# Two hybrid transformer blocks on one core: the compressed branch and the gates between the q, k, v units, the mixing norm's root applied by the consumers, two open output units

## The reference, cut to what matters

```python
x = x + 0.5 * swiglu_ffn(rmsnorm(x, ffn1_norm_g), ffn1_w_in, ffn1_w_out)
h = rmsnorm(x, mix_norm_g)
q, kv, nsa_g, conv_in, q_mem, merge_g = jnp.split(h @ w_in, split_points, axis=-1)
q = rmsnorm(q.reshape(b, s, N_HEADS, HEAD_DIM), q_norm_g)
kc, vc, ks, vs, kw, vw = [t.reshape(...) for t in jnp.split(kv, 6, axis=-1)]
k_cmp = rmsnorm(compress(kc, cmp_pe_k, cmp_w1_k, cmp_w2_k), k_norm_g)   # silu((blocks + pe) @ w1) @ w2
v_cmp = compress(vc, cmp_pe_v, cmp_w1_v, cmp_w2_v)
gates = jax.nn.sigmoid(nsa_g)
o_nsa = nsa_attention(q, k_cmp, v_cmp, rmsnorm(ks, k_norm_g), vs, rmsnorm(kw, k_norm_g), vw, gates, rel_bias)
o_conv = short_gated_conv(conv_in, conv_w, conv_b)     # gate_b * (conv3(gate_c * x_in) + conv_b)
o_mem = memory_attention(q_mem, mem, ...)
g_nsa, g_conv, g_mem = jnp.split(jax.nn.sigmoid(merge_g), 3, axis=-1)
x = x + (g_nsa * o_nsa + g_conv * o_conv + g_mem * o_mem) @ w_out
x = x + 0.5 * swiglu_ffn(rmsnorm(x, ffn2_norm_g), ffn2_w_in, ffn2_w_out)
```

## Time and profile before

| | |
|---|---|
| median of 3 runs | 2926.3 us (2925.95 to 2928.32) |
| the profiled execution | 2924.95 us |
| its span in the profile | 2923.1 us |
| TensorE matmul busy | 2858.3 us, 98% of the span |
| VectorE, ScalarE, GpSimd busy | 1254.6, 1156.1, 1110.9 us |
| mean granted TensorE clock | 0.991 of full |

### The profile page before, as it was taken

One profiled execution on the slowest core, in us unless ns is written; L12 is line 12 of the kernel. 1 busy time (PEld: TensorE's weight loads), 2 busy tenths in 40 slices (PEclk: granted clock), 3 DMA queues, 4 the chain that ended last, 5 costly groups with the idle time before them and its releaser, 6 DMA issues.

```text
span 2923.1 us, 33800 instructions
## 1 busy us (share of the span) xinstructions
PE 2858.3 (98%) x13586; PEld 2282.5 (78%) x13586; DVE 1254.6 (43%) x2039; ACT 1156.1 (40%) x1817; POOL 1110.9 (38%) x506
## 2 busy tenths in 40 slices
PE   8999989899999999999999999999999899999999
PEld 6888867777777887888887777888887567888887
DVE  4333244354555246333334435433337555533323
ACT  4232233355654453322224544332235455332323
POOL 3444433022224524444432213444443333444443
PEclk9999999899999999999999999999999999999999
DMA  4443232122212312222321112223322242222322
GB/s 146 152 137 125 93 111 87 51 82 78 83 65 101 114 61 93 95 100 97 109 83 58 58 51 80 94 101 105 107 86 87 81 129 94 94 101 95 118 91 80
DMA packets 83364, 275.55 MB, mean 94 GB/s; under 512 B 14183, under 2 KB 20583, under 8 KB 82568
## 3 DMA queue, kind: packets, MB, share of 16 engines
q1 hardware_dynamic: 73292, 257.10, 25.7%
q0 software_dynamic: 9440, 15.16, 1.5%
q10 hardware_dynamic: 476, 1.12, 0.1%
HBM read 271.13 MB, written 10.58 MB: 96 GB/s over the span
## 4 chain that ended last, share of the span: by engine, by line
PE 89%; DVE 6%; ACT 3%; issue 1%; DMA 1%; SPq 0%; POOL 0%; DVEq 0%; ACTq 0%
PE bank L442 20%; PE bank L443 20%; PE bank L444 20%; PE bank L597 5%; PE bank L601 5%; PE bank L599 5%; PE bank L624 1%; PE bank L829 1%; PE bank L663 1%; PE bank L651 1%; DVE tmp L1620 1%; PE bank L798 1%; PE bank L968 1%; DMA raw<-in_w 1%; PE bank L859 1%
## 5 line engine op out<-in xcount | busy, mean ns | idle before, releaser
L2178 POOL TENSOR_TENSOR w_lo<-raw,w_hi 128x1024 fp32r<-128x1024 f32 (+1 forms) x423 | 1073.5, 2541 | 1656.6 <-ACT w_hi L1119 1656.6
L1119 ACT ACTIVATE w_hi<-raw 128x1024 fp32r<-128x1024 f32 (+1 forms) x424 | 469.5, 1108 | 1267.2 <-PE bank L444 1133.8
L442 PE MATMUL bank<-a_hi,w_hi 128*128 128x512 f32 x1760 | 696.4, 396 | 19.5 <-DVE a_lo L1602 7.2
L444 PE MATMUL bank<-a_lo,w_hi 128*128 128x512 f32 x1760 | 686.9, 390 | 0.0
L443 PE MATMUL bank<-a_hi,w_lo 128*128 128x512 f32 x1760 | 686.9, 390 | 0.0
L442 PEld LDWEIGHTS bank<-a_hi,w_hi 128*128 128x128 f32 x1760 | 331.7, 188 | 101.1 <-issue 12.2
L443 PEld LDWEIGHTS bank<-a_hi,w_lo 128*128 128x128 f32 x1760 | 331.6, 188 | 71.9 <-issue 4.5
L444 PEld LDWEIGHTS bank<-a_lo,w_hi 128*128 128x128 f32 x1760 | 331.6, 188 | 69.2
L597 PE MATMUL bank<-a_hi,w_hi 128*128 128x512 f32 x704 | 284.7, 404 | 1.9 <-issue 0.8
L601 PE MATMUL bank<-a_lo,w_hi 128*128 128x512 f32 x704 | 282.2, 401 | 0.0
L599 PE MATMUL bank<-a_hi,w_lo 128*128 128x512 f32 x704 | 277.2, 394 | 0.0
(11 more groups left out here) (314 smaller groups left out, 3475.1 us busy)
## 6 DMA issues: line engine op xcount, KB each, us to landing
raw<-in_w SPq DMA_DIRECT2D x360, 512.0 KB, 3.4
raw<-in_w SPq DMA_DIRECT2D x64, 704.0 KB, 4.0
bias_rows<-bias_table POOLq DMA_DIRECT2D x4, 2048.0 KB, 29.4
strip<-bias_rows SPq DMA_DIRECT2D x16, 448.0 KB, 4.2
cw<-in_cw POOLq DMA_DIRECT2D x4, 1024.0 KB, 5.5
terms<-forget_cumsum SPq DMA_DIRECT2D x8, 512.0 KB, 8.0
terms<-forget_cumsum SPq DMA_DIRECT2D x8, 384.0 KB, 6.7
x<-in_x_t SPq DMA_DIRECT2D x4, 512.0 KB, 7.6
```

Source lines behind the costliest of these rows:

```text
L442: mm(dst, high[:, w], hi[:, kbase + b], start=start and b == 0, stop=False)
L444: last = mm(dst, high[:, w], lo[:, kbase + b], start=False, stop=stop and b == nk - 1)
L1119: act(w_hi[v % 3][:, 0:nk * P], raw[v % 5][:, 0:nk * P], ACT.Copy).then_inc(sem("w_hi_ready"), 1)
L2178: eng.tensor_tensor(w_lo[v % 5][:, 0:nk * P], raw[v % 5][:, 0:nk * P], w_hi[v % 3][:, 0:nk * P].bitcast(F32), ALU.subtract).then_inc(sem(" ...
```

## The change

It has five parts.

1. **Norm.** `updated` and `update` of `ffn0_out` get the norm name "mix": VectorE writes x·gain, ScalarE `a_hi` and VectorE `a_lo` in the update of each chunk. The root stays in `rstd`, and every consumer multiplies its tile by it on VectorE: the q, k, v and `cc` tiles, the gates, the convolution tiles, `qmem`, `gnsa` and `gmem`. The root of the memory norm moves to `raw_t[1]`, and so does the square of `rstd` for the convolution.
2. **Order.** The stage `qkv0` is written out by hand in `block_qkv` on each engine, with `cc` tiles first, and the host lays the weights in that order. The two hidden layers of `compress` and its small matmuls stand between the units.
3. **Gates.** They are computed transposed: 24 matmuls of 512 columns with 48 weight columns, sigmoid, and four small transposes.
4. **Position term.** Two operations of 128x992 with two tensor inputs in place of 16 of 128x124.
5. **Output units.** `wo0` opens two units: 21 matmuls of the first, 21 of the second, then the rest.

```diff
+                project_tile(0)
+                second = unit_steps(u + 1, bank[1][:, :], a_hi, a_lo)
+                advance(second, 9)
+                mean("mix")
+                advance(second)
+                for t in range(2, 4):
+                    project_tile(t)
+                hidden(0)
+                project_tile(4)
+                key_raw()
+                project_tile(5)
+                head_mean(0)
+                key_mean()
+                project_tile(6)
+                head_mean(1)
+                hidden(1)
+                project_tile(7)
...
+                def hidden(kv):
                     eng.wait_ge(sem("xc_ready"), kv + 1)
+                    if kv == 1:
+                        eng.wait_ge(sem("kcmp_done"), 2)
...
+                def gate_raw():
+                    eng.wait_ge(sem("wg_split"), 1)
+                    eng.wait_ge(sem("vcmp_done"), 2)
+                    for b in range(NCH):
+                        w = slice(b * 48, (b + 1) * 48)
+                        mm(bank[7][0:48, :], wg_hi[:, w], a_hi[:, b], start=b == 0, stop=False)
...
+            def merged_out():
...
+                first, second = out(0), out(1)
+                advance(first, 21)
+                advance(second, 21)
+                advance(first)
+                advance(second)
+                for k in range(2, NCH):
+                    advance(out(k))
...
-            mean("mix")
-            project("qkv0", a_hi, a_lo, parts=split_base["mix_norm"])
-            small(v0["qmem"], wg_hi, wg_lo, 48, "wg_split", "gates_raw")
-            compress()
+            block_qkv()
             nsa()
...
-                updated(f"ffn{f}_out", (None, "attn0", "ple0", "ple1")[f])
+                updated(f"ffn{f}_out", ("mix", "attn0", "ple0", "ple1")[f])
...
-                        eng.wait_ge(sem("unit_done"), u + t + 1)
+                        if name == "qmem":
+                            eng.wait_ge(sem("qmem_seen"), t + 1)
+                        else:
+                            eng.wait_ge(sem("unit_done"), u + t + 1)
                         act(act_t[sq % 2][:, 0:n], bank[t % 4][:, 0:n], ACT.Square).then_inc(sem("square_ready"), 1)
...
+                        if name == "qmem":
+                            wait("unit_done", u + t + 1)
+                            eng.tensor_tensor(b[:, 0:n], b[:, 0:n], rstd[:, :], ALU.mult).then_inc(sem("qmem_seen"), 1)
+                        if ended:
+                            normed()
                         group.append(t)
...
+                for g in range(2, 5):
+                    seen(g)
+                    normed(g - 1)
+                eng.tensor_tensor(rstd_twice[:, :], rstd[:, :], rstd[:, :], ALU.mult)
+                gate_seen()
...
+                def conv_gate(c):
+                    wait("unit_done", u + 4 * c + 1)
+                    eng.tensor_tensor(cb[:, :], bank[6][:, :], rstd[:, :], ALU.mult).then_inc(sem("conv_taken_even"), 1)
+
+                def conv_gate_seen(c):
+                    wait("unit_done", u + 4 * c + 4)
+                    eng.tensor_tensor(bank[7][:, :], bank[7][:, :], rstd[:, :], ALU.mult).then_inc(sem("conv_gate_seen"), 1)
...
+                    own(eng.tensor_tensor(cu[:, 2:S + 2], cu[:, 2:S + 2], rstd_twice[:, :], ALU.mult))
```

More of the change, by code:

```diff
@@ L335, in build @@
         }
+        block_norms = [t for t, tile in enumerate(tiles["qkv0"]) if tile[0] == "norm"]
+        block_turns = [bank[6], bank[7], bank[7], bank[5]]
         norm0, sq0, v0, g, n, v = {}, {}, {}, 0, 0, 0
@@ L532, in project, with block_qkv, project_tile, head_mean @@
                 post()
[L534 to L552, removed]
+            def block_qkv():
+                u, tk = U0["qkv0"], taken0["qkv0"]
+                def project_tile(t):
+                    eng.wait_ge(sem("tile_taken"), tk + t - 3)
+                    unit(u + t, 0, bank[t % 4][:, :], a_hi, a_lo, K8,
+                         parts=split_base["mix_norm"] if t == 0 else None).then_inc(sem("unit_done"), 1)
+                def head_mean(g):
+                    if g >= 2:
+                        eng.wait_ge(sem("tile_taken"), tk + block_norms[g - 2] + 1)
+                    eng.wait_ge(sem("square_ready"), g + 1)
+                    mm(bank[4 + g % 2][:, :], cst("mean_head"), act_t[g % 2][:, :], start=True, stop=True)\
+                        .then_inc(sem("head_mean"), 1)
+                def hidden(kv):
                     eng.wait_ge(sem("xc_ready"), kv + 1)
+                    if kv == 1:
+                        eng.wait_ge(sem("kcmp_done"), 2)
                     for half in range(2):
@@ L563, in compress @@
                         last.then_inc(sem("cw1_used"), 1)
[L564 to L581, removed]
@@ new lines, in value_raw @@
+                def value_raw():
+                    eng.wait_ge(sem("chid_ready"), 4)
+                    for g in range(4):
+                        for ht in range(2):
+                            last = mm(bank[6 + g % 2][32 * (g % 2):32 * (g % 2) + NCMP, g // 2 * HD:(g // 2 + 1) * HD],
+                                      chid[:, ht, g, :], cw2[:, 1, ht, :], start=ht == 0, stop=ht == 1)
+                    last.then_inc(sem("vcmp_raw"), 1)
+                def gate_raw():
[4 more added lines that the diff above has]
+                        mm(bank[7][0:48, :], wg_hi[:, w], a_hi[:, b], start=b == 0, stop=False)
+                        mm(bank[7][0:48, :], wg_lo[:, w], a_hi[:, b], start=False, stop=False)
+                        last = mm(bank[7][0:48, :], wg_hi[:, w], a_lo[:, b], start=False, stop=b == NCH - 1)
+                    last.then_inc(sem("gates_raw"), 1)
@@ new lines, in block_qkv @@
+                head_mean(3)
+                gate_raw()
+                project_tile(9)
+                head_mean(4)
+                gate_turn()
+                project_tile(10)
+                eng.wait_ge(sem("gates_ready"), 1)
+                block_turn_v(0)
+                project_tile(11)
+                block_turn_v(1)
+                for t in range(12, 19):
+                    project_tile(t)
+                    head_mean(t - 7)
+                project_tile(19)
+                block_turn_v(2)
@@ L1092, in _ @@
             mem_attention()
-            tiles_by_four("wo0", b_hi, b_lo, "x_done", x0["wo0"], split_base["gmem"])
+            merged_out()
             ffn(1, "ffn1")
```

394 lines of the change are left out of this document (277 added, 117 removed).

## The result

The changed kernel takes 2897.23 us (median of 4 runs, 2897.01 to 2897.79), the kernel before 2927.24 (4 runs, 2925.95 to 2928.32). The ratio is 0.9899, with a 95% interval of 0.9884 to 0.9914: 30 us less. The forecast was 2893, in a range of 2885 to 2902. Its net is right, and more so than its parts: one of them came out at nothing, and within another two errors cancelled.

What follows compares the result with a forecast made beforehand. TensorE, working 98% of the span, was taken as the bound, with time to come from its waits, slow stretches and removed work. The terms summed to -33.0 us, giving a forecast of 2893 us in a range of 2885 to 2902.

Steps and rivals of the forecast that it cites:

- Mixing norm, -16.0: From ffn0_out's last matmul to unit 1: 22.3 us shrink to 6.32, one unit and one mean without idle time.
- Gates, -17.3: Gate matmuls: 23.1 us including the wait become 24 matmuls at 5.44 plus about 0.3 for four small transposes.
- Compressed branch, -2.7: Both hidden layers and small matmuls: 24.25 us become 21.5, including a new 3.9 us stall before the second layer.
- the rival in which it falls to the low clock: First hidden layer's 64 matmuls take 12.0 us instead of 7.0, plus 1.5 in the unit behind: 2900; chance 0.10.
- v turns, -0.7: Turns of the v tiles between unit 1 and the gates: units now standing between hide most of 0.8 us waiting.
- Output units, -3.9: At wo0, 42 matmuls needing only earlier chunks cover the wait for the last b_lo and its low clock; 0.2 left.
- qmem, +7.6: In qmem, ScalarE's squares wait behind VectorE's 16 memory-input operations: unit 4 comes 4.6 us later, then 3.0 more.
- The rival of held squares: In qmem, VectorE's memory-input squares stay held 2.2 us each, so the head mean comes 4.4 later: 2897; chance 0.10.
- The sentence that the clock falls in every such stall: For PE's stalls: the clock falls in each too, so a removed wait gives back more than its own length.
- nsa and the queues at nothing: nsa's three added VectorE multiplications per chunk hide behind waits for PE; DMA queues issue the same transfers: no cost.

Runs made afterwards that it cites:

- the early `xc`: Changed kernel with VectorE making the values' xc right behind the last cc tile, and wg_lo moved behind kcmp: 2890.05 us.
- `gates_narrow`: Changed kernel with the gates' 24 matmuls of 512 columns replaced by the former 96 of 48 columns, at the new place: 2910.1 us.
- `third_in_norm`: Changed kernel with memory-input squares spread behind qmem multiplications 0 to 2, and multiplication 3 moved behind the first operation of the first pair's norm: 2889.18 us.
- `best`: Changed kernel with spread memory-input squares, early xc, kcmp ahead of wg_lo, multiplication 3 within the norm, and kcmp and vcmp clearings moved earlier: 2882.76 us.
- `combined`: Changed kernel with early xc, all 16 memory-input operations behind the second qmem multiplication, and the position term in 16 operations again: 2893.06 us.

## Why the prediction was right, and where it wasn't

- **Mixing norm, -16.0: right.** No idle time at the mean, and 33 matmuls ahead of it, as priced. Put back ahead of unit 0, the mean alone costs 6.7 of it.
- **Gates, -17.3: nearly.** The 24 matmuls take 5.98 us (460.82 to 466.80) where I had 5.44, and the turns 0.37. The reason given, the wait and the low clock that it brings, was the smaller part of it: without any wait ahead the old shape still took 15.4 us.
- **Compressed branch, -2.7: this step was mis-sized; it came to 0.** The second layer's stall was 5.10, not 3.9, and outside its bounds of 1.7 and 4.5. The chain was the right one, and `wg_lo` was held as assumed; the error is the `xc` pair at 3.6 instead of 2.4. I priced it by width, from contiguous operations. The layer then took 9.55 for 9.05. And the stall of 1.34 ahead of the first layer wasn't in the sum at all. There the `xc` pair (400.79 to 406.5) was held by a `w_lo` for 2.0 us; at 3.68 it would have ended at 404.5, before TensorE was free at 405.2. The layer itself took 7.2, so the rival in which it falls to the low clock did not occur.
- **v turns, -0.7: right.** The three turns inside the block add 0.4 to 0.5 us each, with the unit behind them, and the fourth, now in `nsa`'s first chunk, 0.5: 1.9 us, as the forecast left them, where there were 2.6.
- **The rest of the block.** It took 153.3 us (382.4 to 535.69) where the terms give 149.4. The branch is 2.7 of the 3.9, the gates 0.6; most of the rest lies in units of about 5.6 us instead of 5.44 behind a change of the kind of matmul.
- **Output units, -3.9: right**, -3.6.
- **qmem, +7.6: right in its first mechanism, and in size, 7.7, partly by luck.** 3.48 us at the head mean were forecast as 3.5, and VectorE's operations on the memory input were not held any more. The rival of held squares did not occur. But the 1.3 us of low clock behind that stall were absent: mean and next unit took 7.28 us, and 7.21 before. So unit 4 came 3.7 late and not 4.6, and the second half, 3.0 by a guess between bounds, was 4.0: the new wait of 2.23 at unit 6, and 1.6 of low clock behind it. The two errors cancel. In the second execution of the same kernel the low clock stood behind the head mean and not at unit 6: 4.3 and 2.4, 6.7 in all. The sentence that the clock falls in every such stall was wrong. For the second half the runs gave the place: multiplication 3 behind the first pair's norm.
- **nsa and the queues at nothing: right.**
- **The sum.** -16.0 - 16.8 + 0 - 0.7 - 3.6 + 7.7, with about 0.4 of other small losses, is some -29 us; the profiled executions differ by 27.2, which holds 1.9 of lateness at the start, and the medians by 30.0.

## What to carry to other kernels

When work moves from a chain that everything waits for into each consumer, list what already stands in the consumer engine's program at that point. Here one multiplication per tile, 0.7 us long, cost 6.7 to 7.7 us, because the first ones came to stand behind 16 operations that nobody needed yet, and a later one behind a norm. Moving the 16 in one block only moved the wait to the next tile; spreading them over the gaps, and pulling the later multiplication forward, gave nearly all of it back. Where an instruction with only a late reader (`wg_lo`) stands ahead of one on the path (`kcmp`), swap them: with the early `xc` this gave 7.2 us here.

## What the runs showed of the hardware

- TensorE's clock fell from the full to the half level within 96 matmuls of 48 columns, with no idle time at all: 51 of them in a stretch of 5.4 us at a granted clock of 1.00, then 42 in 8.7 us at 0.50 (`gates_narrow`).
- The price of a stall is not fixed, not even for one program. In two executions of the changed kernel unit 6 waited 2.23 us; it took 7.22 us in one and 5.58 in the other, at granted clocks of 0.76 and 1.00. After 2.54 us unit 4 took 5.56 us in `third_in_norm` and 7.18 in `best`. A single execution can't size such a stall to better than 1.6 us.
- An operation whose input takes every 16th element took 1.8 to 2.0 us for 992 columns when nothing held it, as one of two (3.68 for the pair) or as eight of sixteen (3.68 and 3.83 for the 16 in the kernel before, 3.96 in `combined`). That the stride is the cause was not tested.
- VectorE and GpSimd hold each other: `wg_lo` took 0.56 us alone and 2.65 beside a `w_lo`, and `w_lo` took 2.40 alone and 3.86 behind the first `xc` operation.
